# One decoder layer on one core: the softmax's maximum placed behind the pair's last low halves, ahead of the next pair's sums

## The chip, the cores and the metric

The kernel runs on one core of one Trainium2 chip. The metric is the device time of one execution in microseconds (us). Unless marked ns, all times are in us.

## The reference, cut to what matters

One inference step of a layer with three gated branches over 512 prompt tokens and 8 sample tokens, 1024 channels, float32. Branch C is cross-attention of the prompt into 256 memory tokens with 4 heads of 256 channels:

```python
def cross_attn(c_q, mk, mv):
    lead = c_q.shape[:-1]
    q = c_q.reshape(*lead, C_HEADS, C_HD)
    s = jnp.einsum('bthd,bmhd->bhtm', q, mk).astype(jnp.float32) * (C_HD ** -0.5)
    p = jax.nn.softmax(s, axis=-1).astype(mv.dtype)
    return jnp.einsum('bhtm,bmhd->bthd', p, mv).reshape(*lead, C_WIDTH)
...
    out_c = cross_attn(c_q, mk, mv) * jax.nn.silu(c_z)
```

Two of the input projection's blocks matter here as well: `c_z` (block CZ of the kernel) and the third merge gate (block GC). Each is a 1024 by 1024 weight times the 520 tokens.

## The kernel before, in words

Every float32 product is made from three fp32r products: an operand is split into a high part (ACT copies it into an fp32r tile, names ending in `_hi`) and a low part (DVE subtracts the high part, names ending in `_lo`), and PE adds low by high, high by low and high by high.

The projections run one after the other through one stream of weights, in the order of `NAMES`: ... PA, CZ, GC, PC, OUT. SP loads 256 columns of a weight (1 MB) into one of two `raw` buffers. CZ and GC are the `FAST` blocks: 8 pairs of 128 columns each way, numbered q = 0 to 7, and each pair is done with seven half-sized products P1 to P7 in place of eight (the scheme of Strassen and Winograd). A product is 12 matmuls (4 pieces of the contraction by three). For that, DVE forms sums of weight quarters (`pair_sums`: three additions, for the units S3, S1 and S2; `last_sum`: S4), ACT and DVE split each unit into high and low halves, and ACT copies partial results between PSUM banks (`pair_copy`, `pair_keep`, `pair_five`). DVE adds others (`add_low`, `add_high`). P7 of a pair waits for ACT's `pair_keep` copy of P6's bank, and P4 waits for DVE's `add_low`.

Nothing schedules this at run time. Each engine's order is written out by hand, in one function `pairs(q)` per engine, with semaphores between the engines. `pair_ahead(q + 1, part)` prepares the next pair's weights in three parts. Part 0 is the low half of A11 and the three sums, part 1 the low half of S2, part 2 the low halves of S3, S1 and A12, and the last sum. `hooks` puts the attention between the products, half a head to a pair, so head h spans the pairs 2h and 2h + 1:

- In an even pair, PE computes the head's scores (`att_scores`, 24 matmuls into `p45`) ahead of P6. It turns the probabilities (L1459, eight 128 by 128 transposes) behind P2, in pair 0 behind P7.
- Between these, DVE takes the maximum over the 256 memory tokens (L2332, one reduction of 128 by 1024) and scales it (L2333). ACT takes the exponentials of the four blocks of 128 tokens, each with its sum (L1107). DVE then inverts the sums (L2335) and scales the four blocks (L2337), after which PE may turn them.
- ACT copies the turned probabilities (L1112), DVE subtracts (L2121), and in the odd pair PE multiplies them by the values (`att_pv`, 12 matmuls of 512 columns).

In `before`, DVE's order in an even pair is `add_high(q - 1)` (L1900), `last_lo(q)` (L1870, or two halves), `pair_ahead(q + 1, 0)` (L1853, L1879, L1880, L1881), `att_soft(h)` (L2332 to L2337), `pair_ahead(q + 1, 1)`, `add_low(q)` (L1894), `pair_ahead(q + 1, 2)`. In pair 0, four small copies (L2112) stand ahead of `att_soft`. ACT's order around it is `pair_keep(q)`, which loads the table of the exponential and makes the copy (L999, L1005), then `att_exp(h)` (L1107), then `pair_five(q)` (L1010).

Of the kernel before, what the change touches and what calls it, by code (L numbers as in the profile page):

```python
# [30 lines left out]
NT = T // P  # L31
# [84 lines left out]
def bass_gated_parallel_step(nc, x_prompt, x_sample, state_gla, cache_mem_k, cache_mem_v,  # L116
# [24 lines left out]
    with ExitStack() as ctx:  # L141
# [17 lines left out]
        def sem(name):  # L159
            if name not in sems:  # L160
                sems[name] = ctx.enter_context(nc.semaphore(name))
            return sems[name]
# [179 lines left out]
        def slot(unit, q):  # L342

            return (7 * q + UNIT[unit]) % 8
# [51 lines left out]
        def wait_product(eng, name, q):  # L396

            if name == "P3":
                eng.wait_ge(prod_done, FIRST_TILE + 2 * q + 2)
            else:  # L400
                eng.wait_ge(sem("half_done"), ORDER.index((name, q)) + 1)
# [212 lines left out]
        def _(act):  # L614
# [24 lines left out]
            def mem_squares():  # L639
                act.wait_ge(sem("mem_loaded"), 16)  # L640
                link(square(mem_in[:, 0, :], junk, 5))
                act.wait_ge(sem("x_sq"), 3)
                A(rstd[:, 5:5 + MT], ssq[:, 5:5 + MT], ACT.Sqrt, scale=1.0 / D, bias=eps_col[:, :]).then_inc(sem("rt_x"), 1)

            def mem_hi_part(k):
                act.wait_ge(sem("xT_done"), X_M + k + 1)
                A(x_hi[:, k, 0:MEM], x_bank(X_M + k), ACT.Copy, scale=gm1[:, k:k + 1]).then_inc(sem("xT_hi"), 1)
# [151 lines left out]
            def hooks(name, c):  # L799
                if name == "QK" and c == 1:  # L800
                    mem_squares()
                if name == "QK" and 3 <= c <= 6:
                    mem_hi_part(2 * c - 6)
                    mem_hi_part(2 * c - 5)
                if name == "V" and c == 0:
                    act.wait_ge(sem("gd_done"), 1)
                    for i in range(4):
                        ins = A(gdT_hi[:, i * Q4:(i + 1) * Q4], p67[32 * i:32 * i + RANK, 0, 0:Q4], ACT.Copy)
                    ins.then_inc(sem("gdT_ready"), 1)
                    act.wait_ge(sem("up_loaded"), 16)  # L810
                    A(up_hi[:, :], up_raw[:, :], ACT.Copy).then_inc(sem("gdT_ready"), 1)
                if name == "V" and c == 7:
                    gla_abs(0)
                if name == "BV" and c == 0:
                    gla_abs(1)
                if name == "BV" and c == 2:
                    act.wait_ge(sem("z_abs"), 2 * BH)
                    A(zabs, zabs, ACT.Exp, scale=-1.0).then_inc(sem("zln"), 1)
                if name == "BV" and c == 3:
                    act.wait_ge(sem("zln"), 1)  # L820
                    A(zabs, zabs, ACT.Ln, bias=1.0).then_inc(sem("zln"), 1)
                q = KT * (BLK[name] - BLK["BZ"]) + c
                if 4 <= q < 4 + 3 * NT and q % 3 == 1:
                    gla_exps_carried((q - 4) // 3)
                if 5 <= q < 5 + 3 * NT and q % 3 == 2:
                    gla_split_hi((q - 5) // 3)
                if name == "GB" and c == 1:
                    gla_out_hi(NT - 1)
                    A(egs, decay[:, :, T:TT], ACT.Exp, scale=TRI).then_inc(sem("samples_act"), 1)
                if name == "AZ" and c == 3:  # L830
                    act.wait_ge(sem("samples_dve"), 4)
                    A(x_hi[:, :, T:TT], mz[:, :, T:TT], ACT.Copy).then_inc(sem("samples_act"), 1)
                if name == "AU" and c == 2:
                    decode_exp()
                if name == "AU" and c == 3:
                    ln_roots()
                if name == "GA":
                    act.wait_ge(sem("mix_ready"), c + 1)
                    A(x_hi[:, c, :], t1[:, c, :], ACT.Copy).then_inc(sem("mix_hi"), 1)
                if name == BEFORE and 3 <= c <= 5:  # L840
                    t_hi(c - 3)
                u = KT * (BLK[name] - BLK["CZ"]) + c
                if 0 <= u < 16:
                    h, step = divmod(u, 4)
                    if step == 0:
                        att_exp(h)
                    if step == 1:
                        att_p(h)
                    if step == 2:
                        if h < CH - 1:  # L850
                            att_hi(h + 1)
                        att_out(h)
                    if u == KT + 1:
                        act.wait_ge(sem("oc_parts"), 3)
                        A(x_hi[:, :, T:TT], t1[:, :, T:TT], ACT.Copy).then_inc(sem("oc_hi"), 1)
# [11 lines left out]
            def gla_abs(a):  # L867

                act.wait_ge(sem("z_done"), a + 1)
                for h in range(BH):  # L870
                    A(zabs[:, h, 2 * Q4 * a:2 * Q4 * (a + 1)], z_bank[h], ACT.Abs, bias=bgc[:, h:h + 1]).then_inc(sem("z_abs"), 1)
# [124 lines left out]
            def pair_keep(q):  # L996

                if q % 2 == 0:
                    A(table, eps_col, ACT.Exp)  # L999
                wait_product(act, "P6", q)  # L1000
                if q == 0:
                    act.wait_ge(stage_used, ST["PA"] + KT)
                else:
                    act.wait_ge(sem("pair_added"), 2 * q)
                A(u2_copy, banks(q)[1], ACT.Copy).then_inc(sem("pair_copied"), 1)  # L1005
# [93 lines left out]
                act.wait_ge(sem("att_loaded"), 48 * (h + 1))  # L1099
                A(v_hi[:, :, :], v_raw, ACT.Copy).then_inc(sem("ap_hi"), 1)  # L1100

            def att_exp(h):
                act.wait_ge(sem("anmx"), h + 1)
                if h == 0:
                    act.wait_ge(sem("docs_done"), 1)
                for n in range(NT):
                    A(prob[:, n, :], p45_4[:, n, :], ACT.Exp, scale=C_SCALE, bias=nmx[:, n:n + 1],  # L1107
                      accum_out=den[:, n:n + 1]).then_inc(sem("aexp"), 1)

# [691 lines left out]
        def _(dve):  # L1801
# [64 lines left out]
            def last_lo(q):  # L1866

                dve.wait_ge(hi_ready, FIRST_TILE + 2 * q + 2)
                if slot("S4", q) < 7:
                    ins = V.tensor_tensor(both(w_lo_units, "S4", q), raw_both(q, 1), f32(both(w_hi_units, "S4", q)), ALU.subtract)  # L1870
                else:
                    V.tensor_tensor(unit_of(w_lo_units, "S4", q), raw_part(q, "S4"), f32(unit_of(w_hi_units, "S4", q)), ALU.subtract)
                    ins = V.tensor_tensor(unit_of(w_lo_units, "A22", q), raw_part(q, "A22"), f32(unit_of(w_hi_units, "A22", q)), ALU.subtract)
                ins.then_inc(split_done, 2)
# [27 lines left out]
            def pair_ahead(q, part):  # L1902

                if q == PAIRS:
                    if part == 0:
                        lo(FIRST_TILE + 2 * PAIRS, 0)
                    elif part == 2:
                        lo(FIRST_TILE + 2 * PAIRS + 1, 1)
                elif part == 0:
                    unit_lo("A11", q)  # L1910
                    pair_sums(q)
                elif part == 1:
                    unit_lo("S2", q)
                else:
                    sums_lo(q)
                    unit_lo("A12", q)
                    last_sum(q)

            def pairs(q):

                name, p = FAST[q // 4], q % 4
                if q == 0:
                    att_lo(0)
                    t_lo(3)
                if q > 0:
                    add_high(q - 1)
                last_lo(q)
                pair_ahead(q + 1, 0)
                hooks(name, 2 * p)
                pair_ahead(q + 1, 1)  # L1930
                add_low(q)
                pair_ahead(q + 1, 2)
                hooks(name, 2 * p + 1)
                if q == PAIRS - 1:
                    add_high(q)
# [391 lines left out]
                    dve.wait_ge(sem("ap_hi"), 3 * h + n + 1)  # L2327
                    V.tensor_tensor(dst, src, f32(top), ALU.subtract).then_inc(sem("ap_lo"), 1)

            def att_soft(h):  # L2330
                dve.wait_ge(sem("asc_done"), h + 1)
                link(V.tensor_reduce(mx, p45_4, AX_X, ALU.max))  # L2332
                V.tensor_scalar(nmx, mx, -C_SCALE, None, ALU.mult).then_inc(sem("anmx"), 1)  # L2333
                dve.wait_ge(sem("aexp"), NT * (h + 1))
                link(V.reciprocal(rden, den))  # L2335
                for n in range(NT):
                    V.tensor_scalar(prob[:, n, :], prob[:, n, :], rden[:, n:n + 1], None, ALU.mult).then_inc(sem("ap_ready"), 1)  # L2337
# [188 lines left out]
```

## Time and profile before

| what | value |
|---|---|
| median of 3 runs | 859.04 us (858.25 to 860.0) |
| the profiled execution | 858.57 us |
| its span in the trace | 856.7 us |
| PE busy | 837.1 us (98%) |
| PE waiting for DVE's scaled probabilities, by the trace | 4.8 us in 4 waits |
| PE waiting for `add_low`, by the trace | 3.9 us in 4 waits |

Busy is the time in which an engine had an instruction running. The span runs from the first to the last instruction of the trace, and the execution's own time is 1.9 us more. Matmuls overlap in the pipeline: one that is shown with 0.28 us is followed by the next after 0.12 us, so lengths are read from start to start.

### The profile page before, as it was taken

How to read it: one execution, taken by the hardware profiler on the slowest of the kernel's cores; microseconds unless marked ns; L12 is line 12 of the kernel's file. 1: busy time of each engine (PE TensorE's matmuls, PEld its weight loads, DVE VectorE, ACT ScalarE, POOL GpSimd, SP SyncE). 2: the span in 40 equal slices, each digit the busy share in tenths (PEclk: the TensorE clock that was granted, in tenths of full speed). 3: DMA queues.
4: the chain of work that ended last, by engine and by line, in shares of the span. 5: the costliest groups of instructions: out<-in, count | busy, mean ns of one | idle time of the engine just before them, and what ended most of it. 6: DMA issues, size and time to landing. Idle time of an engine off the chain costs nothing.

```text
span 856.7 us, 16406 instructions
## 1 busy us (share of the span) xinstructions
PE 837.1 (98%) x6827; PEld 812.6 (95%) x6827; DVE 484.9 (57%) x828; ACT 401.1 (47%) x691; POOL 67.6 (8%) x122
## 2 busy tenths in 40 slices
PE   8999999999999999999999999999998998999997
PEld 7999999999999999999999999999887898999995
DVE  6527542735464385313327797546778788745534
ACT  7534446348766543422232253333347767743424
POOL 1001000000000222001012111001120000000000
PEclk9999999999999999999999999999999999999999
DMA  9324743331322859524267864316543341262402
GB/s 301 100 87 151 256 148 100 99 101 51 122 75 86 255 189 347 182 98 140 85 222 267 279 196 151 100 52 244 198 178 117 99 148 50 73 239 71 136 1 101
DMA packets 87206, 126.22 MB, mean 147 GB/s; under 512 B 3114, under 2 KB 73816, under 8 KB 87136
## 3 DMA queue, kind: packets, MB, share of 16 engines
q1 hardware_dynamic: 73328, 76.58, 27.8%
q0 software_dynamic: 13712, 48.57, 16.4%
q8 instruction: 53, 0.87, 0.4%
q14 instruction: 17, 0.14, 0.1%
q10 hardware_dynamic: 96, 0.06, 0.0%
HBM read 112.98 MB, written 12.22 MB: 146 GB/s over the span
## 4 chain that ended last, share of the span: by engine, by line
PE 87%; DVE 6%; ACT 4%; issue 1%; DMA 1%; SPq 0%; ACTq 0%; DVEq 0%
PE mm L1313 54%; PE mm L1270 5%; PE mm L1285 5%; PE mm L1350 3%; PE mm L1259 3%; PE mm L1603 2%; PE mm L1685 2%; PE p L1244 1%; PE mm L1624 1%; PE mm L1623 1%; PE mm L1622 1%; PE p L1562 1%; PE p L1532 1%; DMA raw<-in_w_in_dram 1%; PE p L1246 1%
## 5 line engine op out<-in xcount | busy, mean ns | idle before, releaser
L1819 DVE TENSOR_TENSOR w_lo<-raw,w_hi 128x1024 fp32r<-128x1024 f32 x114 | 138.7, 1220 | 84.9 <-ACT w_hi L631 83.7
L1313 PE MATMUL mm<-h_lo,w_hi 128*128 128x260 f32 (+1 forms) x832 | 170.1, 286 | 0.0
L1313 PE MATMUL mm<-h_hi,w_hi 128*128 128x260 f32 (+1 forms) x832 | 167.4, 283 | 0.0
L1313 PE MATMUL mm<-h_hi,w_lo 128*128 128x260 f32 (+1 forms) x832 | 167.2, 282 | 0.0
L1313 PEld LDWEIGHTS mm<-h_lo,w_hi 128*128 128x128 f32 x832 | 128.0, 188 | 2.5 <-issue 2.4
L1313 PEld LDWEIGHTS mm<-h_hi,w_hi 128*128 128x128 f32 x832 | 128.1, 188 | 0.0
L1313 PEld LDWEIGHTS mm<-h_hi,w_lo 128*128 128x128 f32 x832 | 128.1, 188 | 0.0
L631 ACT ACTIVATE w_hi<-raw 128x1024 fp32r<-128x1024 f32 x114 | 118.9, 1052 | 12.0 <-DMA raw<-in_w_mem_kv_dram 6.3
L1313 PE MATMUL mm<-x_lo,w_hi 128*128 128x260 f32 (+1 forms) x448 | 96.2, 284 | 0.0
L1313 PE MATMUL mm<-x_hi,w_hi 128*128 128x260 f32 (+1 forms) x448 | 95.3, 283 | 0.0
L1313 PE MATMUL mm<-x_hi,w_lo 128*128 128x260 f32 (+1 forms) x448 | 95.1, 282 | 0.0
L1313 PEld LDWEIGHTS mm<-x_lo,w_hi 128*128 128x128 f32 x448 | 71.2, 188 | 2.6 <-issue 2.6
L1313 PEld LDWEIGHTS mm<-x_hi,w_hi 128*128 128x128 f32 x448 | 71.2, 188 | 0.0
L1313 PEld LDWEIGHTS mm<-x_hi,w_lo 128*128 128x128 f32 x448 | 71.1, 188 | 0.0
L780 ACT ACTIVATE stage<-mm 128x520 f32<-128x520 f32 x24 | 14.5, 605 | 76.8 <-PE mm L1313 76.8
L1350 PE MATMUL mm<-h_lo,w_hi 128*128 128x260 f32 x128 | 38.2, 298 | 3.9 <-DVE stage L1894 3.9
L1350 PE MATMUL mm<-h_hi,w_lo 128*128 128x260 f32 x128 | 37.5, 293 | 0.0
L1350 PE MATMUL mm<-h_hi,w_hi 128*128 128x260 f32 x128 | 37.4, 292 | 0.0
L1285 PE MATMUL mm<-w_hi,h_lo 128*128 128x256 f32 x128 | 36.7, 286 | 0.0
L1270 PE MATMUL mm<-h_lo,w_hi 128*128 128x264 f32 x128 | 36.6, 286 | 0.0
L1270 PE MATMUL mm<-h_hi,w_lo 128*128 128x264 f32 x128 | 36.3, 283 | 0.0
L1270 PE MATMUL mm<-h_hi,w_hi 128*128 128x264 f32 x128 | 36.3, 283 | 0.0
(446 smaller groups left out, 1769.3 us busy)
## 6 DMA issues: line engine op xcount, KB each, us to landing
raw<-in_w_in_dram SPq DMA_DIRECT2D x43, 1024.0 KB, 5.4
raw<-in_w_branch_dram SPq DMA_DIRECT2D x12, 1024.0 KB, 5.1
raw<-in_w_mem_kv_dram SPq DMA_DIRECT2D x8, 1024.0 KB, 5.9
gate<-in_cache_mem_k_dram POOLq DMA_DIRECT2D x16, 512.0 KB, 6.3
tok<-in_cache_mem_v_dram POOLq DMA_DIRECT2D x14, 512.0 KB, 5.4
tok<-in_state_gla_dram POOLq DMA_DIRECT2D x8, 512.0 KB, 7.4
out_dram<-tok POOLq DMA_DIRECT2D x8, 512.0 KB, 7.2
work<-scr_q POOLq DMA_DIRECT2D x8, 512.0 KB, 5.0
```

The source lines that it names most:

```text
L631: A(w_hi[:, j], raw[:, j // 2, :, (j % 2) * P:(j % 2 + 1) * P], ACT.Copy).then_inc(hi_ready, 1)
L780: ins = A(st, src, ACT.Copy)
L1244: MM(out, w[0], x[1], start=first_mm, stop=False)
L1246: return MM(out, w[0], x[0], start=False, stop=last_mm)
L1259: ins = MM(mm[:, j // 2, n, 0:2 * P], xp[:, k, ns], wp[:, j - 1:j + 1, k, :], start=(k == 0 and xp is x_lo), stop=(k == KT - 1 and xp is x ...
L1270: ins = MM(mm[:, j % 2, 0, 0:TT - 256], wp[:, j, k, :], xp[:, k, 256:TT], start=(k == 0 and xp is h_lo), stop=(k == KT - 1 and wp is w_hi ...
L1285: ins = MM(mm[:, n, 1, 0:2 * P], xp[:, k, n * P:(n + 1) * P], wp[:, j - 1:j + 1, k, :], start=(k == 0 and xp is h_lo), stop=(k == KT - 1 a ...
L1313: ins = MM(mm[:, j % 2, a, 0:c1 - c0], wp[:, j, k, :], xp[:, k, c0:c1], start=(k == 0 and wp is w_hi and xp is xl), stop=(k == KT - 1 and ...
L1350: last = MM(out, wp[:, k, :], xp[:, k, :], start=(first_mm and k == 0 and xp is xl), stop=(k == KH - 1 and wp is wh and xp is xh), skip_gr ...
L1603: ins = MM(o_bank[j % 4][:, 0:TT - 256], wp, xp[:, k, 256:TT], start=(k == 0 and xp is h_lo), stop=(k == KT - 1 and last))
L1685: ins = MM(mm[:, j % 2, j // 2, 0:c1 - c0], wp[:, j, k, :], xp[:, k, c0:c1], start=(k == 0 and xp is h_lo), stop=(k == KT - 1 and wp is w_ ...
L1819: V.tensor_tensor(w_lo[:, j], raw[:, j // 2, :, (j % 2) * P:(j % 2 + 1) * P], f32(w_hi[:, j]), ALU.subtract).then_inc(split_done, 1)
```

## The change

`att_soft` on DVE is cut in two. `att_max(h)`, the maximum and its scaling, now runs directly behind `last_lo(q)` of the even pair, ahead of `pair_ahead(q + 1, 0)`. The rest (the inversion and the four scalings) stays where it was. On ACT, the first of the four exponentials moves into `pair_keep(q)`, between the table load and the wait for P6 ahead of the copy. The other three stay behind the copy. No instruction is added or removed, and PE, POOL and SP keep their order.

```diff
@@ ACT hooks
                     if step == 0:
-                        att_exp(h)
+                        att_exp(h, 1, 2, 3)
@@ ACT pair_keep
                 if q % 2 == 0:
                     A(table, eps_col, ACT.Exp)
+                    att_exp(q // 2, 0)
                 wait_product(act, "P6", q)
@@ ACT att_exp
-            def att_exp(h):
+            def att_exp(h, *blocks):
+
                 act.wait_ge(sem("anmx"), h + 1)
                 if h == 0:
                     act.wait_ge(sem("docs_done"), 1)
-                for n in range(NT):
+                for n in blocks:
@@ DVE pairs
                 last_lo(q)
+                if q % 2 == 0:
+                    att_max(q // 2)
                 pair_ahead(q + 1, 0)
@@ DVE att_max, att_soft
-            def att_soft(h):
+            def att_max(h):
+
                 dve.wait_ge(sem("asc_done"), h + 1)
                 link(V.tensor_reduce(mx, p45_4, AX_X, ALU.max))
                 V.tensor_scalar(nmx, mx, -C_SCALE, None, ALU.mult).then_inc(sem("anmx"), 1)
+
+            def att_soft(h):
+
                 dve.wait_ge(sem("aexp"), NT * (h + 1))
                 link(V.reciprocal(rden, den))
```

DVE in pair 2 (head 1), before. L1870 is `last_lo(2)`, L1853 to L1881 prepare pair 3:

```order
L1870 TENSOR_TENSOR w_lo<-raw,w_hi 128x1024 [waits hi_ready]
L1853 TENSOR_TENSOR w_lo<-raw,w_hi 128x512 [waits unit_hi]
L1879 TENSOR_TENSOR raw<-raw 128x4x128 [waits unit_lo]
L1880 TENSOR_TENSOR raw<-raw 128x4x128 [waits dve_link]
L1881 TENSOR_TENSOR work<-raw 128x512
L2332 TENSOR_REDUCE small<-p 128x4 [waits asc_done]
L2333 TENSOR_SCALAR small<-small 128x4 [waits dve_link]
L2335 RECIPROCAL small<-small 128x4 [waits aexp]
```

The same place with the change (L1872, L1855, L1881, L1882, L1883, L2337, L2338 and L2343 are the lines of the same instructions):

```order
L1872 TENSOR_TENSOR w_lo<-raw,w_hi 128x1024 [waits hi_ready]
L2337 TENSOR_REDUCE small<-p 128x4 [waits asc_done]
L2338 TENSOR_SCALAR small<-small 128x4 [waits dve_link]
L1855 TENSOR_TENSOR w_lo<-raw,w_hi 128x512 [waits unit_hi]
L1881 TENSOR_TENSOR raw<-raw 128x4x128 [waits unit_lo]
L1882 TENSOR_TENSOR raw<-raw 128x4x128 [waits dve_link]
L1883 TENSOR_TENSOR work<-raw 128x512
L2343 RECIPROCAL small<-small 128x4 [waits aexp]
```

The maximum and its scaling went from behind the four preparing instructions to ahead of them. They now stand between the maximum and the inversion.

ACT in pair 2, before. L999 is the table load, L1005 `pair_keep`'s copy, L1010 `pair_five`:

```order
L999 ACT_TABLE_LOAD
L999 ACTIVATE small<-small 128x1
L1005 ACTIVATE stage<-mm 128x260 [waits pair_added,half_done]
L1107 ACTIVATE work,small<-p,small 128x256 [waits anmx]
L1107 ACTIVATE work,small<-p,small 128x256 x3
L1010 ACTIVATE stage<-mm 128x260 [waits half_done]
```

The same place with the change:

```order
L999 ACT_TABLE_LOAD
L999 ACTIVATE small<-small 128x1
L1109 ACTIVATE work,small<-p,small 128x256 [waits anmx]
L1006 ACTIVATE stage<-mm 128x260 [waits pair_added,half_done]
L1109 ACTIVATE work,small<-p,small 128x256 [waits anmx]
L1109 ACTIVATE work,small<-p,small 128x256 x2
L1011 ACTIVATE stage<-mm 128x260 [waits half_done]
```

One exponential, with its wait for the maximum, went ahead of the copy that P7 waits for.

## Rows read from the trace of the kernel before

**Rows 1.** The page: busy time, share and instructions of each engine.

```profile
PE 837.1 (98%) x6827; PEld 812.6 (95%) x6827; DVE 484.9 (57%) x828; ACT 401.1 (47%) x691; POOL 67.6 (8%) x122
```

**Rows 2.** Waits of PE from 640 us on: total, times, longest.

```profile
PE p L1459 <- DVE work L2337: 4.8, 4, 3.1
PE mm L1350 <- DVE stage L1894: 3.9, 4, 1.8
```

**Rows 3.** DVE's timeline in pair 2 (start, length, engine, line).

```profile
671.69 0.69 DVE L1853 TENSOR_TENSOR w_lo<-raw,w_hi 128x512 fp32r<-128x512 f32 x1
...
674.35 1.22 DVE L2332 TENSOR_REDUCE small<-p 128x4 f32<-128x1024 f32 x1
...
677.77 0.18 DVE L2335 RECIPROCAL small<-small 128x4 f32<-128x4 f32 x1 [2.00 <-ACT work L1107]
```

**Rows 4.** ACT's timeline in pair 2.

```profile
673.60 0.39 ACT L1005 ACTIVATE stage<-mm 128x260 f32<-128x260 f32 x1 [0.81 <-PE mm L1350]
675.80 0.48 ACT L1107 ACTIVATE work<-p,small 128x256 f32<-128x256 f32 x1 [1.82 <-DVE small L2333]
```

**Rows 5.** PE's timeline in pair 2, round the turning.

```profile
677.61 0.28 PE L1350 MATMUL mm<-h_hi,w_hi 128*128 128x260 f32 x1
678.39 0.33 PE L1459 MATMUL p<-ident,work 128*128 128x128 f32 x1 [0.51 <-DVE work L2337]
679.37 0.37 PE L1350 MATMUL mm<-h_lo,w_hi 128*128 128x260 f32 x1
```

**Rows 6.** PE's timeline in pairs 0 and 1, head 0.

```profile
641.47 0.28 PE L1246 MATMUL p<-k_hi,x_hi 128*128 128x256 f32 x1
...
645.76 0.28 PE L1350 MATMUL mm<-t_hi,w_hi 128*128 128x260 f32 x1
649.18 0.30 PE L1459 MATMUL p<-ident,work 128*128 128x128 f32 x1 [3.14 <-DVE work L2337]
650.91 0.56 PE L1350 MATMUL mm<-h_lo,w_hi 128*128 128x260 f32 x1 [0.59 <-DVE stage L1894]
...
656.56 0.39 PE L1244 MATMUL p<-pT_lo,v_hi 128*128 128x512 f32 x1
```

**Rows 7.** DVE's timeline in pair 0.

```profile
642.06 0.69 DVE L1853 TENSOR_TENSOR w_lo<-raw,w_hi 128x512 fp32r<-128x512 f32 x1 [1.18 <-ACT w_hi L956]
...
645.05 1.21 DVE L2332 TENSOR_REDUCE small<-p 128x4 f32<-128x1024 f32 x1
...
648.47 0.18 DVE L2335 RECIPROCAL small<-small 128x4 f32<-128x4 f32 x1 [2.00 <-ACT work L1107]
648.68 0.35 DVE L2337 TENSOR_SCALAR work<-work,small 128x256 f32<-128x256 f32 x1
```

**Rows 8.** Stretches: length, busy PE, PEld, DVE, ACT, POOL; then PEclk, DMA, GB/s.

```profile
650.91:653.65 2.74, 2.74 (x13) 2.74 (x14) 2.71 (x4) 2.28 (x3) 0.00 (x0) 0.50 0.03 9
726.00:728.00 2.00, 2.00 (x11) 2.00 (x11) 0.95 (x2) 0.87 (x2) 0.00 (x0) 0.50 0.02 4
```

**Rows 9.** PE's timeline where P4 of pairs 1 and 5 starts.

```profile
666.15 0.36 PE L1350 MATMUL mm<-h_lo,w_hi 128*128 128x260 f32 x1 [0.90 <-DVE stage L1894]
...
724.67 0.36 PE L1350 MATMUL mm<-h_lo,w_hi 128*128 128x260 f32 x1 [1.84 <-DVE stage L1894]
```

**Rows 10.** End of P3(4) on PE; ACT behind it in pair 5.

```profile
712.24 0.28 PE L1350 MATMUL mm<-h_hi,w_hi 128*128 128x260 f32 x1
...
712.72 0.26 ACT L855 ACTIVATE x_hi<-t 128x64 fp32r<-128x64 f32 x1 [1.42 <-DVE t L2134]
...
713.95 1.05 ACT L976 ACTIVATE w_hi<-raw 128x1024 fp32r<-128x1024 f32 x1
```

**Rows 11.** PE where head 3 is multiplied by the values.

```profile
743.67 0.28 PE L1350 MATMUL mm<-h_hi,w_lo 128*128 128x260 f32 x1
743.79 0.28 PE L1350 MATMUL mm<-h_hi,w_hi 128*128 128x260 f32 x1
744.16 0.50 PE L1244 MATMUL p<-pT_lo,v_hi 128*128 128x512 f32 x1
```

## The prediction

> **What bounds the kernel now.** The page comes first: PE is busy 98% of the span [rows 1]. An edit that leaves PE's own work alone can only gain where PE waits, or where its clock is low. The list of waits comes second. From 640 us on it shows two kinds of any size: PE waits four times for L2337, the scaled probabilities, 4.8 us in all and 3.1 in the longest, and four times for L1894, `add_low`, 3.9 us in all [rows 2]. Both kinds lie in the eight pairs that the change touches. Third come the timelines of PE, DVE and ACT round those waits, and last the granted clock, which is 0.50 (1.2 of 2.4 GHz) in two stretches, behind the two longest waits [rows 8].
>
> The timelines show a chain between DVE and ACT. In pair 2, DVE's low half of A11 and the three sums run from 671.69 to 674.35, the maximum starts at 674.35, ACT's first exponential at 675.80, and DVE's inversion at 677.77, after 2.00 us with nothing else on DVE [rows 3, 4]. PE has finished its four products by then: the last matmul starts at 677.61, the first transpose only at 678.39 [rows 5]. In pair 0 only three products cover the softmax, and PE's gap is from 645.76 to 649.18 [rows 6]. So DVE idles while ACT works on the exponentials, and PE waits for both. The change fills DVE's idle time with the sums.
>
> **The change, step by step.** It has the same instructions, so there is nothing to add or take off for work. What moves is when each starts. One product is 12 matmuls. From start to start one takes 0.12 us [rows 11], so a product takes 1.44.
>
> Head 1, pair 2. The maximum now waits for the scores instead of standing behind the sums. ACT's copy starts when P6 ends, 673.60 [rows 4]. One product earlier the scores are done: 672.16. DVE is free at 671.69 [rows 3], so it waits 0.47 with the sums queued behind. Nobody wants those sums before ACT splits S2, which ACT does only behind its exponentials. From the maximum to the first exponential it takes 675.80 - 674.35 = 1.45, so that exponential starts at 673.6. DVE goes on with 2.66 us of A11 and sums (674.35 - 671.69) and reaches the inversion at 676.3, 1.5 earlier. The exponentials take 1.97 in all (677.77 - 675.80), and with ACT's copy in between they end at 675.9, so DVE no longer waits. The first transpose comes 0.62 behind the inversion (678.39 - 677.77): 676.9. PE would be ready 0.12 behind the matmul of 677.61, at 677.73, so PE's wait goes, with 0.85 to spare. Worth: 678.39 - 677.73 = **0.7 us**. What is late next is PE itself.
>
> The price is on ACT: the copy for P7 now stands behind one exponential. It starts at 673.6 + 0.48, takes 0.39 and ends at 674.5. P7 starts two products behind the start of P6, about 674.8. I cost it at nothing. The cover is 0.3 us thin; without it each head loses what is missing.
>
> Head 0, pairs 0 and 1. The last matmul of the scores starts at 641.47 and takes 0.28, so the maximum starts at 641.8, inside 1.18 us in which DVE was idle [rows 6, 7]. It takes 1.42 with its scaling, then come the sums and four small copies, 645.05 - 642.06 = 2.99, and the inversion is at 646.2 in place of 648.47 [rows 7]. Everything on DVE behind it follows, `add_low` too, and P4(0) waits for that. Worth: **2.3 us**. PE still waits here, some 0.9 us for the transposes and 0.6 for P4(0).
>
> The clock. PE runs 650.91 to 653.65 at 1.2 GHz, behind waits of 3.14 and 0.59 us [rows 6, 8]. The 36 matmuls from 650.91 to 656.56 take 5.65 us where 36 x 0.12 = 4.3 would do. A wait of 0.90 did not bring the clock down, one of 1.84 did [rows 8, 9]. With 0.9 and 0.6, parted by the eight transposes, I am nearer to the first: the fall goes. Worth: **1.3 us**, with 0 as the other end. What is gained up to the end of P3(0) stays, since ACT's and DVE's chain for the odd pair starts from P3's end; the wait of 0.90 ahead of P4(1) stays too.
>
> The Trainium skill, page "TensorE: Matmul & The Clock Gate", Part 1, says that the monitor behind the clock runs freely and does not start with the kernel. By that rule the same waits bring a fall in one execution and none in another, in either kernel; one trace can't show it.
>
> Head 2, pairs 4 and 5. At the transposes it is as head 1. But in pair 5 PE waits 1.84 ahead of P4(5) [rows 9], and there ACT is late: P3(4) ends at 712.5, ACT splits S4 and A22 (L976) only at 713.95, since it comes from the probabilities by way of L855, which waited for DVE [rows 10]. That chain starts from the inversion, which is 1.5 earlier; P3(4) ends 0.7 earlier, at 711.8, and L976 would start at 712.4, still later. So the whole shift counts: **1.5 us**. The wait ahead of P4(5) shrinks to about 1.4, between 0.90 and 1.84, and I leave its clock fall as it was. If that goes, 15 matmuls or so at 0.10 more each give 1.5 us more.
>
> Head 3, pairs 6 and 7. 0.7 as in head 1. Also PE starts on the values 744.16 - 743.79 = 0.37 behind the matmul before, 0.25 over the usual, because DVE's L2121 was late [rows 11]; that is 1.4 earlier now. In heads 1 and 2 this is lost again ahead of P4, in pair 7 P4 had no wait, so it counts. Worth: **1.0 us**.
>
> Sum: 2.3 + 1.3 + 0.7 + 1.5 + 1.0 = 6.8. The profiled execution took 858.57, so 851.8. The median of the runs lies 0.47 above it: **852.2 us**. A difference of 0.2% (1.7 us) is about what a measurement of this kernel can tell from none.
>
> **The rivals.**
> - The second clock fall goes too: 852.2 - 1.5 = 850.7. For it: the wait ahead of P4(5) loses a quarter. Against: 1.4 us is no nearer to 0.90 than to 1.84.
> - The first fall stays: 852.2 + 1.3 = 853.5. For it: two waits of 1.5 us together within three. Against: each is no longer than the one of 0.90.
> - The odd pairs take it back: PE comes early from heads 1 and 2 and waits the longer for `add_low` in pairs 3 and 5: 852.2 + 0.7 + 1.5 = 854.4. It decides if `last_lo` of those pairs starts no earlier than now. For it: PE waits there today [rows 9]. Against: that chain starts from P3 or from the inversion, and both are earlier.
> - Slower: two engines now wait for the scores with other work behind them, DVE ahead of the sums, ACT ahead of P7's copy. If the maximum starts only with P6's end, 1.44 later than I say, the copy in pair 2 ends at 675.9 and P7 starts 1.1 late; the transposes start at 678.8, 0.45 later than today, in three heads. Head 0 gains 0.8 and keeps its low clock. That alone is 859.5. From a start 0.4 later still, at every head, P7 loses that too, four times: 861. It decides from a maximum that starts about 1.8 us behind the scores. Against it: ACT and DVE start within 0.1 us of PE's last matmul in today's rows [rows 4], so only something new could do it.
> - The Trainium skill, same page, Specifications, calls ScalarE's and VectorE's queues strict first-in, first-out. That is this rival's mechanism, and the trace agrees: nothing ran on DVE in the 2.00 us ahead of L2335 [rows 3].
> - No change: the inversion still waits, since ACT's exponentials come no earlier: 859.0.
>
> **How the numbers follow.** Forecast 0.48, second fall gone too 0.20, first fall stays 0.12, odd pairs take it back 0.10, a mixture of smaller losses (P7 waits some 0.3 at each head, 853 to 856) 0.03, no change 0.04, slower 0.03. Faster by over 0.2%: 0.93; within 0.2%: 0.04; slower: 0.03. The range goes from 850.0, the better clock case less the runs' spread of 0.8, to 855.4, the odd-pair case plus about 1.
>
> **What the profile of the changed kernel would show.** PE's waits for the scaled probabilities: one of 0.9 in pair 0, none in pairs 2, 4 and 6. The maximum starts within 0.1 us of the scores' end, some 0.5 behind `last_lo`. The inversion no longer waits for ACT in pairs 2, 4 and 6. The first exponential stands ahead of L1006's copy and P7 does not wait. The granted clock is full in pair 1. The wait ahead of P4(1) is still 0.9, that of P4(5) is about 1.4. The prediction is wrong if P7 waits for the copy, if the maximum starts late, or if the time won in pairs 2 and 4 comes back as longer waits ahead of P4(3) and P4(5).

## The result, and the profile after

| | before | changed |
|---|---|---|
| median | 858.64 us (856.18 to 860.0, 4 runs) | 849.54 us (849.14 to 851.16, 4 runs) |
| ratio, 95% interval | | 0.9897 (0.988 to 0.9913) |
| span of the profiled execution | 856.7 | 849.2 |
| PE busy | 837.1 | 833.5 |
| PE waiting for scaled probabilities | 4.8 in 4 waits | none listed |
| PE waiting for `add_low` | 3.9 in 4 waits | 3.9 in 4 waits |
| PE waiting for A11's low half in pair 0 | none listed | 0.7 |

The change gains 9.1 us of median. I had forecast 852.2 with a range from 850.0: the direction is right, the size is not, and the time lies 0.46 us below the range. One execution of e2 (1018.99 us, clock 0.751) and one of before in its job (906.23 us, clock 0.849) ran in the chip's slower state and are left out of the medians below.

The two largest waits of PE from 640 us on, in the changed kernel, answer to [rows 2] (two more, of 0.4 and 0.3, stand in both kernels). The columns are the total, the number of waits and the longest.

```profile
PE mm L1352 <- DVE stage L1896: 3.9, 4, 1.5
PE mm L1352 <- DVE w_lo L1855: 0.7, 1, 0.7
```

The wait for L2337 (now L2345) is gone. The wait of 1.84 for `add_low` (now L1896) has become 1.45. A new wait of 0.7 stands in pair 0.

DVE's timeline in pair 2 of the changed kernel answers to [rows 3]:

```profile
668.42 1.23 DVE L1872 TENSOR_TENSOR w_lo<-raw,w_hi 128x1024 fp32r<-128x1024 f32 x1 [0.81 <-ACT w_hi L976]
...
670.03 1.23 DVE L2337 TENSOR_REDUCE small<-p 128x4 f32<-128x1024 f32 x1 [0.38 <-PE p L1248]
...
671.37 0.68 DVE L1855 TENSOR_TENSOR w_lo<-raw,w_hi 128x512 fp32r<-128x512 f32 x1
...
674.02 0.17 DVE L2343 RECIPROCAL small<-small 128x4 f32<-128x4 f32 x1
```

ACT beside it, to [rows 4]:

```profile
671.49 0.48 ACT L1109 ACTIVATE work<-p,small 128x256 f32<-128x256 f32 x1 [0.83 <-DVE small L2338]
...
671.96 0.38 ACT L1006 ACTIVATE stage<-mm 128x260 f32<-128x260 f32 x1
```

DVE waits 0.38 us for PE's scores ahead of the maximum, and the inversion (L2343) no longer waits. From the start of `last_lo` (668.42) to the inversion (674.02) there are 5.60 us. Before, there were 7.22: the same, plus 2.00 of waiting, less the 0.38. So the inversion comes 1.62 earlier. ACT's copy for P7 (L1006) starts 0.47 us behind the first exponential, and PE lists no wait for it.

PE's timeline at the places where heads and waits begin, changed kernel (start, length):

```profile
643.15 0.28 PE L1352 MATMUL mm<-t_lo,w_hi 128*128 128x260 f32 x1
...
645.42 0.39 PE L1352 MATMUL mm<-h_lo,w_hi 128*128 128x260 f32 x1 [0.69 <-DVE w_lo L1855]
...
648.40 0.27 PE L1461 MATMUL p<-ident,work 128*128 128x128 f32 x1
...
650.10 0.36 PE L1352 MATMUL mm<-h_lo,w_hi 128*128 128x260 f32 x1 [0.59 <-DVE stage L1896]
...
654.47 0.39 PE L1246 MATMUL p<-pT_lo,v_hi 128*128 128x512 f32 x1
...
691.79 0.36 PE L1352 MATMUL mm<-h_lo,w_hi 128*128 128x260 f32 x1 [0.92 <-DVE stage L1896]
...
720.08 0.36 PE L1352 MATMUL mm<-h_lo,w_hi 128*128 128x260 f32 x1 [1.45 <-DVE stage L1896]
...
731.62 0.27 PE L1461 MATMUL p<-ident,work 128*128 128x128 f32 x1
...
736.79 0.40 PE L1246 MATMUL p<-pT_lo,v_hi 128*128 128x512 f32 x1
...
842.77 0.40 PE L1626 MATMUL mm<-x_hi,h_hi 128*128 128x512 f32 x1
```

The same marks of before stand in [rows 6, 9, 11]. Four are not among the rows: P6(0), P4(3), head 3's transposes and the last matmul.

```profile
641.58 0.28 PE L1350 MATMUL mm<-t_lo,w_hi 128*128 128x260 f32 x1
...
694.77 0.36 PE L1350 MATMUL mm<-h_lo,w_hi 128*128 128x260 f32 x1 [0.53 <-DVE stage L1894]
...
738.54 0.33 PE L1459 MATMUL p<-ident,work 128*128 128x128 f32 x1 [0.61 <-DVE work L2337]
...
850.26 0.40 PE L1624 MATMUL mm<-x_hi,h_hi 128*128 128x512 f32 x1
```

From mark to mark:

| stretch of PE | before | changed | difference |
|---|---|---|---|
| P6(0) to P4(0), head 0's softmax | 9.33 | 6.95 | -2.38 |
| P4(0) to the values of head 0 | 5.65 | 4.37 | -1.28 |
| to P4(3), head 1 | 38.21 | 37.32 | -0.89 |
| to P4(5), head 2 | 29.90 | 28.29 | -1.61 |
| to head 3's transposes | 13.87 | 11.54 | -2.33 |
| to the values of head 3 | 5.62 | 5.17 | -0.45 |
| to the last matmul | 106.10 | 105.98 | -0.12 |
| sum | | | -9.06 |

The two spans differ by 7.5 and not by 9.06. P6(0) starts 1.57 later in the profiled execution of the changed kernel, and that is ahead of everything that the change touches. Near 100 us a weight landed late, ACT waited for it, and PE after it:

```profile
99.46 1.06 ACT L631 ACTIVATE w_hi<-raw 128x1024 fp32r<-128x1024 f32 x1 [2.81 <-DMA raw<-in_w_mem_kv_dram]
```
```profile
102.97 0.39 PE L1261 MATMUL mm<-w_hi,x_lo 128*128 128x256 f32 x1 [1.35 <-DVE w_lo L1821]
```

The list of before has no such wait of PE. That execution took 851.16 us; the other three, 849.14 to 849.61. The same wait of 1.3 stands in the profile of e1, and one of 1.1 in that of e9.

Last, the clock, to [rows 8]. The number behind POOL's "(x0)" is the granted clock. It is 1.00 (2.4 GHz) both behind P4(0) and behind P4(5), where before had 0.50 (1.2 GHz). A stretch at 1.2 GHz is called a fall below.

```profile
650.10:652.96 2.86, 2.86 (x24) 2.86 (x25) 2.83 (x4) 2.83 (x5) 0.00 (x0) 1.00 0.02 6
720.08:723.00 2.92, 2.92 (x24) 2.92 (x25) 2.27 (x3) 0.88 (x2) 0.00 (x0) 1.00 0.00 0
```

### The profile page after: what moved, and what is told of

It reads as the page before. It is cut to its first block, busy times and chain, and to the rows that moved or that the text cites. A ratio compares the mean times of both kernels' runs of the same rounds, so it can differ in the third digit from the quotient of the medians.

```text
span 849.2 us, 16407 instructions
## 1 busy us (share of the span) xinstructions
PE 833.5 (98%) x6827; PEld 810.7 (95%) x6827; DVE 484.8 (57%) x828; ACT 401.4 (47%) x691; POOL 67.7 (8%) x122
## 4 chain that ended last, share of the span: by engine, by line
PE 90%; DVE 5%; DMA 2%; ACT 1%; issue 1%; SPq 0%; ACTq 0%; DVEq 0%
PE mm L1315 54%; PE mm L1352 6%; PE mm L1272 6%; PE mm L1287 5%; PE mm L1605 2%; PE mm L1687 2%; PE mm L1261 1%; DMA raw<-in_w_mem_kv_dram 1%; PE p L1246 1%; PE p L1248 1%; PE p L1247 1%; PE mm L1626 1%; PE mm L1625 1%; PE mm L1624 1%; PE p L1564 1%; PE p L1534 1%
```

## The experiments

Three questions were open. Which of the two edits carries the gain? Does a low clock cost time, and why did both falls go, where I had kept one? And is what is left ahead of P4 a matter of order?

Below, "clock" is the mean granted clock of a whole execution. The profiles that show two falls in the eight pairs have 0.995, those that show one have 0.996 or 0.997, and those with none 0.998 or 0.999. The last digits carry something else too: behind PE's last matmul the clock falls in the traces, where it costs nothing, and how long that lasts before the end differs. In e8, whose clock is 0.998, PE has no instruction in this stretch:

```profile
840.00:842.00 2.00, 0.00 (x0) 0.00 (x0) 0.00 (x0) 0.00 (x0) 0.00 (x0) 0.50 0.70 261
```

So in an execution without a profile the clock suggests a fall in the pairs, and is good evidence only where the time agrees.

### One edit at a time (e1, e2)

```diff
 e1, from the changed kernel
-                        att_exp(h, 1, 2, 3)
+                        att_exp(h, 0, 1, 2, 3)
...
                     A(table, eps_col, ACT.Exp)
-                    att_exp(q // 2, 0)
 e2, from the changed kernel
                 last_lo(q)
-                if q % 2 == 0:
-                    att_max(q // 2)
...
                     if step == 0:
+                        att_max(h)
                         att_soft(h)
```

> Only DVE's half of the change: the maximum behind last_lo, all four exponentials behind ACT's copy for P7 as before. Theory A (the gain comes from the sums filling DVE's wait for ACT, and from the two clock falls that go with the shorter waits): ACT has the same copy and four exponentials ahead of the inversion either way, so the inversion in pair 2 comes at most 0.3 us later than with the whole change, and PE has over that to spare. Time as with the whole change, 8 to 9.5 us below before. Theory B (the first exponential ahead of the copy carries a good part): 2 us or more of the gain are missing.

Measured: 850.91 us (849.27 to 851.14, 4 runs), before in the same job 858.73; ratio 0.9906 (0.9885 to 0.9927). From P6(0) to the values of head 3 PE takes 93.67 us (642.85 to 736.52), with the whole change 93.64, before 102.58. So in the eight pairs the two kernels are the same, and DVE's half of the change is all of it. The 1.4 us between the medians are the size of the spread that late weights make: three of e1's four executions lie at 850.9 to 851.1, as the one of the changed kernel with the late weight does. Theory A holds, theory B falls. ACT's exponential ahead of the copy is worth nothing, because ACT does four exponentials and one copy ahead of the inversion in either order: from `last_lo` to the inversion e1 has the same 5.60 us.

> Only ACT's half of the change: the first exponential ahead of the copy for P7, the maximum still behind the sums. Theory A: this is my slower rival made real. In pair 2 of before the maximum's scaling ends at 675.8, so the copy ends at 676.7 and P7 starts some 1.9 us late; the transposes start 1.2 us later in heads 1 to 3 and at about the same time in head 0: 3.6 us slower, and up to 5 us more if these waits bring the clock down. 2.5 to 9 us slower than before. Theory B: faster than before, since the exponentials start as early as they can.

Measured: 859.89 us (858.53 to 861.28, 9 runs) against 858.73; ratio 1.0014 (1.0002 to 1.0027), slower by about 1.2. From P6(0) to the values of head 3 the trace has 103.74 us in place of 102.58, again 1.2 more. The waits of PE in e2:

```profile
PE mm L1352 <- ACT stage L1006: 8.4, 4, 2.9
PE mm L1352 <- DVE stage L1896: 2.7, 3, 0.9
```

The mechanism is as expected: P7 waits for ACT's copy at each head. P7(2) waits 1.8, where I had 1.9:

```profile
675.82 0.36 PE L1352 MATMUL mm<-t_lo,w_hi 128*128 128x260 f32 x1 [1.80 <-ACT stage L1006]
```

The size lies below what I expected, 1.2 against 2.5 to 9. I had the transposes later, but left out that their own waits (4.8 in all) would go and that those for `add_low` would shrink (3.9 to 2.7, the one ahead of P4(5) from 1.84 to 0.91). So the order inside ACT is harmless only together with the early maximum. The Trainium skill, page "TensorE: Matmul & The Clock Gate", table of specifications under the title, calls ScalarE's queue strict first-in, first-out. e2 agrees and shows the price, 8.4 us of waits on PE: P6's finished result waiting on ACT behind an exponential whose maximum is not there.

### The clock (e3, e4, e5, e12)

e3 to e5 are the kernel before with matmuls of the identity by itself, whose results nobody reads, in PE's waits. e3, e4:

```diff
 e3, hooks of PE, head 0, ahead of the transposes
                             pe.wait_ge(sem("oc_parts"), 2)
+                            for _ in range(26):
+                                MM(p67[:, 0, 0:P], ident[:, :], ident[:, :], start=True, stop=True)
 e4, pairs of PE
                     product("P1", q)
+                    if q == 6:
+                        for _ in range(13):
+                            MM(p67[:, 0, 0:P], ident[:, :], ident[:, :], start=True, stop=True)
                     product("P4", q - 1)
```

> Kernel before, with 26 matmuls of 128 by 128 whose result nobody reads put into PE's wait of 3.1 us ahead of head 0's transposes (2.9 us of work, it should end before the probabilities are there). DVE and ACT are untouched. Theory A: the granted clock stays full in pair 1, P4(0) to the end of P6(1) takes 4.4 us in place of 5.65, time 1.3 us below before. Theory C (the low clock there costs nothing, something else limits): time as before.

Measured: 858.65 (10 runs) against 858.73; ratio 0.9999 (0.9987 to 1.0012). The experiment was mis-sized, and its median can't tell the theories apart. The trace shows 52 instructions for the 26 matmuls:

```profile
647.16 5.96 PE L1457 MATMUL p<-ident 128*128 128x128 f32 x52
```

The transposes start at 652.96, 2.5 us later behind P6(0) than in before, and P4(0) starts 1.6 late. That eats the gain. But the stretch behind P4(0) ran at full clock, 4.38 us in place of 5.65. The second fall, whose wait e3 leaves as it was, is missing in this profile too:

```profile
726.23 0.35 PE L1350 MATMUL mm<-h_lo,w_hi 128*128 128x260 f32 x1 [1.84 <-DVE stage L1896]
```
```profile
726.23:729.11 2.88, 2.88 (x24) 2.88 (x25) 2.28 (x3) 0.88 (x2) 0.00 (x0) 1.00 0.00 0
```

From there to head 3's transposes it takes 12.31 us, in before 13.87.

> Kernel before, with 13 such matmuls (1.4 us) in PE's wait of 1.84 us ahead of P4(5). Theory A: no clock fall at 725 us, time 1.5 us below before in the executions in which before has that fall. Theory C: as before.

Measured: 858.54 (10 runs); ratio 0.9998 (0.9988 to 1.0008). The same fault: P4(5) started 0.89 late, and the stretch to head 3's transposes took 12.32 in place of 13.87. Since e3 has no fall there either, the full clock of this one profile can't be put down to the filling. e5 is both, with 13 and 7 in place of 26 and 13.

> Kernel before with both waits filled, at half the number (each of those matmuls turned out to be two instructions of 0.11 us): 13 in the wait ahead of head 0's transposes (2.9 us) and 7 ahead of P4(5) (1.6 us). Theory A (the clock falls cost time): the granted clock stays full in pairs 1 and 5, 1.3 us gained in pair 1, and 1.5 in pair 5 in those executions in which before has its second fall: 1.3 to 2.8 us below before. Theory C (the clock costs nothing): as before.

Measured: 855.44 (855.2 to 857.04, 5 runs) against 858.62; ratio 0.9967 (0.9954 to 0.998). That is 3.2 us of median. In the trace, P6(0) to head 3's values takes 99.74 us in place of 102.58: 2.84 less, with PE's waits covered and not shortened, and no instruction of DVE or ACT changed. Head 0's part of the gain is here:

```profile
650.47 0.36 PE L1350 MATMUL mm<-h_lo,w_hi 128*128 128x260 f32 x1 [0.59 <-DVE stage L1899]
```
```profile
654.83 0.39 PE L1244 MATMUL p<-pT_lo,v_hi 128*128 128x512 f32 x1
```

4.36 us from P4(0) to the values, 1.29 under before, although P4(0) starts no earlier behind P6(0). All five executions have a clock of 0.998 or 0.999; of the 46 of before in the jobs of the experiments, only two reach 0.998. So the two falls are worth 2.8 us of the 9.1, and theory C falls.

e12 asks why the second fall went. It is the changed kernel with one subtraction of DVE done twice:

```diff
                     dve.wait_ge(sem("ap_hi"), 3 * h + n + 1)
+                    if h == 3 and n == 2:
+                        link(V.tensor_tensor(dst, src, f32(top), ALU.subtract))
                     V.tensor_tensor(dst, src, f32(top), ALU.subtract).then_inc(sem("ap_lo"), 1)
```

> The changed kernel with one instruction of DVE doubled (the low half of the values, 0.75 us) in pair 5: the wait ahead of P4(5) grows from 1.45 to about 2.2 us. Theory A (the length of that wait decides over the clock fall, the rest is chance): 0.75 us slower in executions without the fall and 2.2 us in those with it, and most have it: granted clock 0.997 instead of 0.999. Rival (the fall had gone because the whole stage moved in time): 0.75 slower, clock 0.999.

Measured: 851.57 (850.0 to 851.84, 6 runs), 2.0 us above the changed kernel. In three of the six the clock is 0.996 (851.34, 851.68, 851.68), in the others 0.998 to 1.0 (850.0, 851.45, 851.84). The profiled one has the fall:

```profile
718.81 0.35 PE L1352 MATMUL mm<-h_lo,w_hi 128*128 128x260 f32 x1 [2.17 <-DVE stage L1896]
```
```profile
718.81:720.00 1.19, 1.19 (x9) 1.19 (x10) 1.19 (x2) 0.00 (x0) 0.00 (x0) 0.87 0.00 0
720.00:722.00 2.00, 2.00 (x11) 2.00 (x11) 1.09 (x2) 0.88 (x2) 0.00 (x0) 0.50 0.00 0
```

From P4(5) to head 3's transposes it takes 13.07 us with this fall, 11.54 in the changed kernel. So with a longer wait the fall comes back, by the clock in three of six executions, where the changed kernel and e1 have none in eight. By the rival, that it had gone because the stage moved in time, there should be none here. These are few executions and one profile, so the rival is unlikely but not refuted. By the clock 851.45 and 851.84 have no fall, and lie 1.5 to 1.8 above the 850.0 that has none either. That is the size of a late weight, but no profile shows it.

### Which head, and whether it adds up (e6, e7)

```diff
 e6: only where the head is 0; e7: only where it is 1 or more
-                if q % 2 == 0:
+                if q % 2 == 0 and (q // 2 == 0):
                     att_max(q // 2)
...
+                        if not (h == 0):
+                            att_max(h)
                         att_soft(h)
```

The edit shown is e6's; e7 has `>= 1` in the same places. In both, ACT's first exponential goes ahead of the copy under the same condition.

> The whole change for head 0 alone, heads 1 to 3 as before. Theory A: P4(0) starts 2.4 us earlier and pair 1 keeps its clock, 1.3 more; the wait of 1.84 ahead of P4(5) stays, with or without its clock fall: 3.7 us below before. Rival (the odd pairs take it back): nearer to 2.

Measured: 854.6 (853.13 to 854.84, 5 runs) against 858.62; ratio 0.9949 (0.9936 to 0.9962), 4.0 of median where 3.7 was expected. The five executions fall in two groups, 1.5 us apart: 853.13 and 853.27 with a clock of 0.999 and 1.0; 854.6, 854.77 and 854.84 with 0.997. The profile is of the first group. The wait ahead of P4(5) is the one of before, and no fall follows:

```profile
720.82 0.35 PE L1353 MATMUL mm<-h_lo,w_hi 128*128 128x260 f32 x1 [1.84 <-DVE stage L1897]
...
733.13 0.33 PE L1462 MATMUL p<-ident,work 128*128 128x128 f32 x1 [0.61 <-DVE work L2348]
```
```profile
720.82:723.70 2.88, 2.88 (x24) 2.88 (x25) 2.28 (x3) 0.88 (x2) 0.00 (x0) 1.00 0.00 0
```

12.31 us from P4(5) to the transposes, against 13.87 in before: the same code and the same wait, with the fall or without, 1.56 us apart. This is the clearest reading of what a fall costs, and e3's profile gives the same two numbers. The same wait brings the clock down in some executions and not in others. That agrees with the Trainium skill, page "TensorE: Matmul & The Clock Gate", Part 1, that the monitor behind the clock runs freely and does not start with the kernel. No run here shows the monitor itself.

> The change for heads 1 to 3 alone, head 0 as before. By the two traces: 0.9 by P4(3), 1.6 more by P4(5), 0.8 for head 3's transposes, 0.6 behind them, together 3.9, and 1.5 more if the clock fall behind P4(5) goes with the shorter wait: 3.9 to 5.4 us below before. Rival (the fall goes by chance and not with the wait): 3.9.

Measured: 853.06 (852.28 to 855.23, 6 runs); ratio 0.9941 (0.9927 to 0.9956), 5.6 of median, at the upper end of what was expected. From P6(0) to head 3's values the profile has 97.17 us (641.60 to 738.77), 5.41 under before: 3.9 for the heads, 1.5 for the second fall, which it does not have. Four executions have a clock of 0.996, as the profiled one with head 0's fall alone; two have 0.993 and take 855.2, some 2.2 more. Whether these two fell behind the wait of 1.45 ahead of P4(5) or elsewhere is not shown. e6 and e7 add up to 4.0 + 5.6 = 9.6, and the whole is 9.1: the heads are independent but for where the clock falls.

### Is the rest a matter of order (e8 to e11)

Ahead of P4(0), P4(1), P4(3) and P4(5) PE still waits for `add_low`. On DVE, work that nobody waits for yet stands before it.

```diff
 e9, pairs of DVE, from the changed kernel
-                pair_ahead(q + 1, 1)
                 add_low(q)
+                pair_ahead(q + 1, 1)
 e10: e9, and behind these two
+                if q % 2 == 1:
+                    att_low(q // 2)
 e8: e10, and
                 last_lo(q)
+                if q == 0:
+                    sample_parts()
```

`att_low` is the wait and the subtraction of `x_lo` from the end of the odd pair's hook. `sample_parts` is the four small copies of pair 0's hook. Both are taken out where they stood. e11 is the kernel before with all of e8's moves and without the change. Before in the job of e9 to e12 has a median of 858.38.

> The changed kernel and three more moves on DVE: add_low ahead of the low half of S2, the attention's x_lo (1.2 us) behind it in odd pairs, and pair 0's four small copies ahead of the maximum. Theory A (P4 of pairs 0, 1, 3, 5 waits for add_low alone, 0.6, 0.9, 0.9 and 1.45 us): these waits go, except what ACT's chain from P3 holds back; about 3 us below the changed kernel. Rival (DVE's total between two pairs sets the pace, so order doesn't matter): as the changed kernel.

Measured: 845.28 (844.81 to 848.09, 4 runs); ratio 0.9854 (0.9836 to 0.9872), 13.3 under before and 4.3 under the changed kernel, where about 3 was expected. The rival, that order doesn't matter, falls. No wait for `add_low` is left on the list; of the eight pairs' own waits one remains:

```profile
PE mm L1352 <- DVE w_lo L1855: 0.7, 1, 0.7
```

> The changed kernel with one more move alone: add_low ahead of the low half of S2. Theory A: P4(1), P4(3) and P4(5) start 0.6 us earlier each; in pair 0 the 0.6 won at P4(0) is held back by ACT's chain. 1.8 us below the changed kernel, about 847.8.

Measured: 848.19 (847.07 to 848.84, 4 runs), 1.35 under the changed kernel. In the eight pairs the trace has 91.62 us in place of 93.64, so 2.0 less; expected was 1.8. Its waits:

```profile
PE mm L1352 <- DVE stage L1896: 1.8, 3, 0.8
PE mm L1352 <- DVE w_lo L1855: 0.7, 1, 0.7
```

P4(3) and P4(5) have lost 0.61 each (0.92 to 0.31, 1.45 to 0.84), and the wait of 0.59 ahead of P4(0) is gone. Most of that one came back at P4(1), 0.67 where 0.3 would be left of 0.90.

> That and the attention's x_lo (1.13 us from start to start) behind add_low in the odd pairs, without the early copies. Theory A: what is left of the waits ahead of P4(1), P4(3) and P4(5), 0.3, 0.3 and 0.85 us, goes as well: 1.4 below e9, about the time of the version with the copies moved too (845.3), since in pair 0 the transposes then start when PE is ready, copies or not.

Measured: 845.1 (844.93 to 845.21, 4 runs); ratio 0.9845 (0.9829 to 0.9861). That is 3.1 under e9 where 1.4 was expected; by the trace, P6(0) to head 3's values takes 89.45 us against 91.62 in e9, so 2.2 of the 3.1 are in the pairs, all the waits that e9 had left there (1.8) and a little more. The rest lies ahead of the pairs: P6(0) starts 1.5 later in e9's profile, which has the late weight near 100 us and e10's has not. e9's two shorter executions, 847.07 and 847.56, are 2.0 and 2.5 above e10. e8 and e10 are the same within their spread, and in the pairs (89.47 and 89.45 us), so the early copies add nothing.

> The kernel before, with the three moves (add_low, x_lo, the copies) and without the change. Theory A: the two edits work on different waits; the change is worth here what it was worth before, some 9 us, less the second clock fall (1.5), which goes with the wait ahead of P4(5) either way: 853 to 855.

Measured: 853.72 (852.43 to 855.0, 4 runs); ratio 0.9951 (0.9934 to 0.9967). The change on top of the three moves, e11 to e8, is worth 8.4 us by the medians, where it has 9.1 on its own. In the pairs of the two profiles it is 7.1 (96.61 to 89.47), against 8.9 on its own, of which 2.8 are the clock; e11's profile has no fall in the pairs. So theory A holds, and what the change is worth in waits alone has grown from 6.1 to 7.1. The list of waits of e11 shows what happens without it:

```profile
PE p L1459 <- DVE work L2348: 5.9, 4, 2.8
```

The waits ahead of P4 are gone, and those ahead of the transposes have grown from 4.8 to 5.9 in all, because PE arrives there earlier and DVE does not.

## Why the prediction was right in its direction and too small

- **What bounds the kernel**: right. PE's two kinds of wait and its clock held nearly all that moved.
- **Head 1**: the inversion comes 1.62 earlier (forecast 1.5) and the wait ahead of the transposes goes, as forecast. 0.7 forecast, 0.89 measured. I counted the transposes' start and not their length: from their start to P1 it is 0.79 now where it was 0.98. They no longer start on the first scaled block with the others still to come: in pair 2 the last block is scaled at 675.37, and the first transpose starts at 675.60.
- **Head 0**: 2.3 forecast, 2.38 measured up to P4(0). One place was wrong. I wrote that nobody wants the sums before ACT splits S2, but in pair 0 P1(1) wants the low half of A11, which stands in the same part. PE waits 0.69 there and no longer 0.9 ahead of the transposes. It cost nothing, since DVE set the pace either way.
- **The first clock fall**: 1.3 forecast, 1.28 measured, and e5 has 1.29 with nothing but the wait filled. That it would go was argued from one trace; e11's profile has no fall behind a wait of 2.82, so a shorter wait is not the only way for it to be missing.
- **Head 2**: 1.5 forecast, 1.61 measured, by the chain named. The inversion starts at 706.37 in before and at 701.77 in the changed kernel, L976 7.58 us behind it in both, P4(5) 18.30 and 18.31 behind it. The wait ahead of P4(5) is 1.45 (forecast 1.4). So the whole shift of the inversion counts, and the shorter transposes add nothing here.

```profile
706.37 0.18 DVE L2335 RECIPROCAL small<-small 128x4 f32<-128x4 f32 x1 [2.00 <-ACT work L1107]
```
```profile
701.77 0.17 DVE L2343 RECIPROCAL small<-small 128x4 f32<-128x4 f32 x1
...
709.35 1.05 ACT L976 ACTIVATE w_hi<-raw 128x1024 fp32r<-128x1024 f32 x1
```

- **The second clock fall**: this is the step that failed. "I leave its clock fall as it was": it went, in all four executions of the changed kernel (clock 0.999 in each), and it is worth 1.56 (e6). This was the first rival, at 850.7, with a chance of 0.20. I held the wait of 1.4 against two readings of one trace, where 0.90 had no fall and 1.84 had one. But 1.84 is itself followed by none in some executions (e3, e6). With the shorter wait and head 0's fall kept (e7), the profiled execution has lost the second fall; with the wait of 1.84 and head 0's fall gone (e6), two of five have. Both hold in the changed kernel. Which weighs more stays open.
- **Head 3**: 1.0 forecast, 1.34 measured without the clock (2.33 + 0.45 + 0.12 - 1.56). The missing part is the shorter transposes (0.19), 0.12 behind the values, and small differences.
- **The odd pairs take it back**: this rival fell. Only the 0.27 that the values started earlier in head 1 was lost again, as the sum said.
- **The slower rival**: its mechanism is real (e2), but not in this change, since the maximum started 0.04 us behind the last matmul of the scores (643.03 + 0.28 to 643.35), far from the 1.8 that this rival wants.
- **The baseline**: the median of before is 858.64 with a fourth run, 0.4 under the one I started from.

By the stretches, the trace gained 9.06 where the sum had 6.8. Of these 2.26 us, 1.56 are the second fall and 0.70 the other terms, 0.34 of them at head 3 and 0.19 at head 1. With 0.4 of the baseline that is 2.66 of the 2.7 us between 852.2 and 849.54. That the median agrees so closely with one pair of profiles is in part luck, since late weights move single executions by 1.5. The range was too narrow below: it took the better clock case less 0.8 for the spread (849.9, written as 850.0), and left nothing for terms that were each a little small.

## What to carry to other kernels

When one engine waits for another's answer, move work that nobody yet waits for into that wait; but look for who wants the *first* piece of it, and keep a wait for a late value out of the queue of an engine that holds an early one. Read a wait on TensorE for two prices, its own length and the low clock behind it; here a low clock followed some waits of 1.80 to 3.14 us and stayed away behind others of 1.80 to 2.82, so compare distributions and clocks of several executions, not one profile. Behind a change that removes one wait, the next is often a matter of order too: here two further moves gave 4.4 us more (e10).

## What was not expected of the hardware

- The same wait of 1.84 us is followed by a stretch at 1.2 GHz in some executions and not in others, 1.56 us apart. In before nearly all executions seem to have both falls: of 46, 42 have a clock of 0.995 or less, two 0.996 and two 0.998 (857.64 and 856.3 us). With head 0's gone the second came in three of five (e6), by clock and time. Why the two come together in before stays open.
- One execution can do both. In e2's profile P7 waits 1.80 us in pair 2, 1.80 in pair 4 and 1.91 in pair 6, and only behind the second does the clock fall:

```profile
675.82:678.70 2.88, 2.88 (x24) 2.88 (x25) 1.58 (x6) 2.88 (x10) 0.00 (x0) 1.00 0.00 0
705.62:708.50 2.88, 2.88 (x14) 2.88 (x15) 1.59 (x6) 2.10 (x9) 0.00 (x0) 0.55 0.00 0
737.02:739.90 2.88, 2.88 (x24) 2.88 (x25) 1.59 (x6) 2.88 (x10) 0.00 (x0) 1.00 0.03 6
```

- The longest wait in the pairs without a fall is in e11, 2.82 us ahead of head 0's transposes, with the full clock from P4(0) on:

```profile
648.61 0.30 PE L1459 MATMUL p<-ident,work 128*128 128x128 f32 x1 [2.82 <-DVE work L2348]
```
```profile
649.73:652.60 2.87, 2.87 (x25) 2.87 (x25) 2.84 (x5) 2.85 (x4) 0.00 (x0) 1.00 0.02 6
```

- The filling matmuls of 128 by 128 in float32 appear as two instructions of 0.11 us each: 26 of them took 5.8 us (e3).
